# The layer norms of the second block's second layer and of the end, with no products of constants ahead of their sums

## The reference

```
h = layer_norm(x, ln_in_g, ln_in_b)
for i in range(2):
    mix = hybrid_mixer(h, ...)
    h = layer_norm(ALPHA * h + mix, ln1_g[i], ln1_b[i])
    ffn = hierarchical_moe(h, ...)
    h = layer_norm(ALPHA * h + ffn, ln2_g[i], ln2_b[i])
return h
```

## Time and profile before

| | us |
|---|---|
| median of 3 runs | 1967.14 |
| runs | 1964.67, 1967.14, 1967.61 |
| profiled execution, first to last instruction (span) | 1964.4 |
| PE busy | 1867.9 (95%) |
| DVE busy | 837.6 (43%) |
| ACT busy | 634.1 (32%) |
| mean share of 16 DMA engines' time (the main queue) | 68.3% |
| mean granted TensorE clock | 0.987 |

### The profile page before, as it was taken

How to read it: one execution, slowest core, us unless ns; L and a number is a source line. 1 busy time by engine, 2 the same in 40 slices (tenths; PEclk the granted TensorE clock), 3 DMA queues, 4 the chain that set the end, 5 groups by cost and what they waited for, 6 DMA issues and landing times. The chain is left out here.

```text
span 1964.4 us, 36047 instructions
## 1 busy us (share of the span) xinstructions
PE 1867.9 (95%) x15650; PEld 1278.5 (65%) x15650; DVE 837.6 (43%) x1699; ACT 634.1 (32%) x1205; POOL 53.1 (3%) x58
## 2 busy tenths in 40 slices
PE   7999999899999999899999999999898999999997
PEld 6889998889997887644444444378785444444443
DVE  5767777767775575511111111155744111111112
ACT  4565554555554341311111111143312111111112
POOL 0500000500000000000000000000000000000000
PEclk9999999999999999999999999999999999999999
DMA  7345554245542329399999999643384999999993
GB/s 286 108 146 188 182 192 168 87 150 193 188 156 83 101 81 387 135 414 427 426 427 427 426 428 426 279 123 121 151 345 195 427 427 426 428 426 426 428 427 140
DMA packets 54241, 540.18 MB, mean 275 GB/s; under 512 B 8608, under 2 KB 9536, under 8 KB 16704
## 3 DMA queue, kind: packets, MB, share of 16 engines
q1 hardware_dynamic: 54080, 537.83, 68.3%
HBM read 536.76 MB, written 1.05 MB: 274 GB/s over the span
## 5 line engine op out<-in xcount | busy, mean ns | idle before, releaser
L2937 PE MATMUL experts_psG<-places_gu,experts_xc 128*64 128x512 f32 x1344 | 297.1, 593 | 5.6 <-DMA places_gu<-in_moe_up 5.6
L511 DVE TENSOR_TENSOR ring_low<-ring_raw,ring_high 128x1024 fp32r<-128x1024 f32 x180 | 222.3, 1245 | 99.9 <-ACT ring_high L505 99.8
L2937 PEld LDWEIGHTS experts_psG<-places_gu,experts_xc 128*64 128x64 f32 x1344 | 96.8, 137 | 198.7 <-issue 185.8
L644 PE MATMUL ffn_ps<-first_x_split,ring_high 128*128 128x512 f32 x616 | 220.6, 396 | 0.3
L2867 DVE SCALAR_TENSOR_TENSOR experts_yc_low<-experts_psD,experts_slot_gate,experts_yc_high 128x512 fp32r<-128x512 f32 x64 | 48.0, 751 | 387.9 <-ACT experts_yc_high L2901 387.9
L505 ACT ACTIVATE ring_high<-ring_raw 128x1024 fp32r<-128x1024 f32 x180 | 186.7, 1051 | 70.6 <-PE ffn_ps L646 30.7
L645 PE MATMUL ffn_ps<-first_x_split,ring_low 128*128 128x256 f32 x704 | 183.4, 281 | 0.0
L2857 DVE TENSOR_TENSOR experts_sig<-experts_sig,experts_psG 128x256 f32<-128x256 f32 x64 | 27.0, 421 | 362.7 <-ACT experts_sig L2889 362.7
L2937 PE MATMUL experts_psG<-weights_gu,experts_xc 128*64 128x512 f32 x704 | 160.4, 608 | 6.7 <-DMA weights_gu<-in_moe_up 6.7
L2889 ACT ACTIVATE experts_sig<-experts_psG 128x256 f32<-128x256 f32 x64 | 24.5, 383 | 416.1 <-PE experts_psG L2937 416.1
L645 PEld LDWEIGHTS ffn_ps<-first_x_split,ring_low 128*128 128x128 f32 x704 | 132.1, 188 | 7.1
(11 more groups left out here) (529 smaller groups left out, 3265.3 us busy)
## 6 DMA issues: line engine op xcount, KB each, us to landing
ring_raw<-in_w SPq DMA_DIRECT2D x90, 1024.0 KB, 4.9
places_gu<-in_moe_gate SPq DMA_DIRECT2D x42, 2048.0 KB, 26.8
places_gu<-in_moe_up SPq DMA_DIRECT2D x42, 2048.0 KB, 28.3
places_d<-in_moe_down SPq DMA_DIRECT2D x32, 2048.0 KB, 24.8
weights_gu<-in_moe_gate SPq DMA_DIRECT2D x22, 2048.0 KB, 25.6
weights_gu<-in_moe_up SPq DMA_DIRECT2D x22, 2048.0 KB, 27.0
weights_d<-in_moe_down SPq DMA_DIRECT2D x16, 2048.0 KB, 25.3
experts_d_more<-in_moe_down SPq DMA_DIRECT2D x16, 2048.0 KB, 26.6
```

What stands on the lines that cost most here:

```text
L511: dve.tensor_tensor(self.low[:, n % AHEAD], self.raw_half(n), self.high[:, n % AHEAD], ALU.subtract)\
L644: pe.matmul(out, w[0][:, kk], f.both[:, :, kk], start=kk == 0, stop=False)
L2937: ins = pe.matmul(out, xc[:, kk], wgu[gu[0]][:, kk, :, j * S:(j + 1) * S], start=kk == 0, stop=kk == DT - 1)
```

## The change

The helper `keep_busy` and its two uses go: four products of constants ahead of the mean's sum and two behind it, in both norms. All else stays, the waits and the order of the other instructions among it.

```diff
     def tensor(pe, between=None):
-        def keep_busy(n):
-
-            for _ in range(n):
-                pe.matmul(psum[:, 1, 0:S], k.c("ones"), k.c("le3")[:, 0:S], start=True, stop=True)
-
         if ln:
-            keep_busy(4)
             pe.wait_ge(folded, 2)
             for t in range(2):
                 ins = pe.matmul(psum[:, 0, 0:S], k.c("ones"), sq[:, 4 + t], start=t == 0, stop=t == 1)
             ins.then_inc(sums, 1)
             if between is not None:
                 between()
-            else:
-                keep_busy(2)
         for t in range(DT):
             pe.wait_ge(squares, t + 1)
```

## The result

The kernel after takes 1971.14 us (median of 22 runs, 1965.20 to 1974.28), the kernel before 1966.87 us (22 runs, 1962.81 to 1972.05). The ratio is 1.0023, with a 95% interval of 1.0016 to 1.0031: the change makes the kernel slower by 4.5 us (3.1 to 6.1); the two medians alone differ by 4.3 us. The forecast was +4.8 us. The profiled execution has a span of 1969.4 us against 1964.4 in the table of before, 5.0 us more.

A forecast was written before the change was run, and what follows sets the result against it. In both norms the engines take turns, so the engine that works was taken as the bound. Squares' sums +1.8 and +1.3 us and projections +1.7 us gave +4.8 us: 1971.9 us, range 1968.0 to 1975.0.

The forecast's parts named there:

- The eight ahead of the mean: In both norms, removal lets the mean start sooner: 0.51 us in the last norm, 0.94 us in the mixers.
- The four behind the mean: In both norms they cost nothing on the path; without them PE pauses about 1.4 us before the first squared tile.
- The squares' sum: In both norms it runs partly at low clock and ends later: +1.8 us in the last norm, +1.3 us in the mixers.
- The projections: Behind the mixers' norm, at L2001, the clock falls after PE's pause of 2.25 us: +1.7 us, bounds 0 and 3.3.
- To the end: From the mixers' norm to the kernel's end, a shift passes whole, as the expert weights do not hide it.
- The sum: Whole kernel: 1.8 + 1.3 + 1.7 = +4.8 us, added to the median of the runs: 1971.9 us.
- The price by throttled time: Both norms and L2001: throttled time times one minus the granted share, pauses or not, estimated at +8.1 us in all.
- Rivals 2 and 5: Norms: full clock back before the squares' sum, 1965.7 us, chance 0.12; clock full through the longer pause, 1963.9, chance 0.03.
- Rival 1: At the projections, L2001, the clock stays full: +3.1 us, 1970.2 us, chance 0.20.
- Rival 3: The clock rises too late for the squares' sums, and L2001 meets a long low stretch: +8.6 us, 1975.7, chance 0.08.
- Rival 4: The mixers' loss does not reach the kernel's end: +1.8 us, 1968.9 us, chance 0.07.

The follow-up runs named there:

- ahead_gone: The kernel before without the four products of constants ahead of the mean's sum, the two behind it kept; measured 1.0004 (0.9995 to 1.0013).
- one_column: The kernel before with the constants' products kept at the same places but 1 column wide in place of 256; measured 1.0025 (1.0012 to 1.0038).
- mixers_gone: The kernel before without the products of constants in the mixers' norm alone; measured 0.9996 (0.9985 to 1.0007), once more 1.0010 (1.0001 to 1.0019).
- after_again: The kernel after, unchanged, run and profiled once more against the kernel before; measured 1.0016 (1.0005 to 1.0026).
- behind_gone: The kernel before without the two products of constants behind the mean's sum, the four ahead kept; measured 1.0000 (0.9989 to 1.0011).
- last_gone: The kernel before without the products of constants in the last norm alone; measured 0.9999 (0.9987 to 1.0010), once more 1.0012 (1.0000 to 1.0025).
- experts_end_filled: The kernel before with four more products of constants at the end of the experts, in PE's pause ahead of both norms; measured 0.9997 (0.9988 to 1.0006).
- mixers_delayed: The kernel before with 32 products of constants behind the squares' sum of the mixers' norm; measured 1.0057 (1.0044 to 1.0070), +11.2 us.

## Why the prediction was right, by its steps

- *The eight ahead of the mean*: right. The pause is 4.46 and 4.85 us, the clock is down when PE resumes, the mean's four products take 2.07 us (1.93 foretold), and the mean comes 0.78 and 0.36 us sooner than before, for 0.94 and 0.51 foretold.
- *The four behind the mean*: it was said that they cost nothing on the path, and that PE pauses 1.4 us without them; both are so (1.43 and 1.42 us). `ahead_gone` shows how much they are worth once the eight are gone.
- *The squares' sum*: the mechanism was right and the size too low. Full clock was taken to be back 4.7 us after the sum's first product; it was 5.99 us (1282.30 to 1288.29) and 5.85 us (1954.87 to 1960.72), just over the upper bound of 5.87 and at it. So the norms cost +2.16 and +2.52 us in place of +1.3 and +1.8; some 0.15 us of either difference is the mean's, which came that much later than foretold. Over the twelve norms without the constants' work, after among them, the distance was 3.2 to 6.0 us, with a mean of 4.8 us; so the profile of after lies at the late end. The 4.7 us were the middle of two bounds and no reading, so that they meet the mean is in part luck.
- *The projections*: right for the profile of after, +1.7 us. With the constants' work gone from the mixers and the pause not filled, the clock fell there in four of five profiles (after, `one_column`, both of `mixers_gone`; not in `after_again`), which is +1.3 us on the mean. With the eight ahead in place it stayed in four of five (before, `behind_gone`, both of `last_gone`; not in `experts_end_filled`), and it stayed in `ahead_gone`. These are few profiles; what decides in a single one is open.
- *To the end*: right, by `mixers_delayed`; in the profile of after the folding of the last norm ends 2.5 us later than before.
- *The sum*: the profile of after has +6.4 us from the three terms for 4.8 foretold, and the other stalls gave 1.3 us of it back. Over all the profiles the terms come to about 1.9 + 2.0 + 1.3 = 5.2 us (1.6 for 1.9 without `mixers_delayed`), within the interval of the measured 4.5 us. The span of the forecast, 1970.2 to 1974.8, does not come out of its own terms, which give 1970.8 (0.8 + 1.2 + 1.7) to 1974.6 (1.9 + 2.3 + 3.3); nothing hangs on it.
- *The price by throttled time* (the Trainium skill, "TensorE: Matmul & The Clock Gate", Terms) would, as an estimate for the stretches that after has, be half of 2 x (10.24 - 3.41) + 3.42, that is 8.5 us. The rows have 6.4 us. Part of each long stretch lies over waits, the folding and the 1.4 us ahead of the squares, and costs nothing; in this profile the measurement decides against the price. The runs do not: the 11.6 us more at 1.2 GHz that they spent on the mean would be 5.8 us by it, again an estimate, and that lies within the measured 3.1 to 6.1.

Rivals 2 and 5 are out: the clock was low when the squares' sum began in every profile without the constants' work. Rival 1 is what `after_again` shows in its profile, 7.14 us at the projections. Rival 3 is out in its second half: the sums came near to its 7.10 us (6.67), but L2001 met a low stretch of 3.42 us, and in no profile a longer one. Rival 4 fell with `mixers_delayed`.

## What to carry to other kernels

A norm or reduction that leaves PE waiting for other engines can lose in its own products as well, since they may run at half clock afterwards (here 3.72 us of products became 5.3 to 6.7 us); look at the granted clock in stretches of some microseconds, as the page's slices do not show it. Work without use on PE pays where it fills a pause in which nothing waits for PE, and it can cost where it stands in the queue ahead of what is needed: in the profile of before the eight products, at half clock, delayed the mean's products by 1.4 and 1.9 us; with eight more put into the pause ahead of them they ran at full clock and delayed the mixers' by 0.2 us (1281.15 against the folding's end at 1280.95). Look at the next pause too, as it can give the gain back (in the profile of `experts_end_filled` the projections did).

## What the runs showed of the hardware that was not expected

The clock that had just come back could be lost again at once. In after it rose at 1288.29 and fell at 1291.70, after a PE pause of 2.24 us; in before PE paused 2.25 us at the same place and it stayed, and in `after_again` it stayed as well, after the same pause as in after. And the same code met the rise at other points from one execution to the next: 5.99 us after the sum in the mixers began in after, 3.20 us in `after_again`. That the point changes from run to run is what the Trainium skill states ("TensorE: Matmul & The Clock Gate", Part 1), and these profiles agree. The 22 runs of after spread over 9 us, twice the effect, and it goes with the clock: the correlation of a run's span with its estimated time at 1.2 GHz is 0.85.
